# Rows of v projected behind the gated values in a one-core decoder trunk, with the long convolution's taps beside them

## The reference

```
mod = silu(c) @ w_ada + b_ada                  # six vectors: shift, scale, gate, twice
h = rms_norm(x) * (1 + sc1) + sh1
q, k, v, B, C, D = split(h @ w_in)             # nine column groups of 256
ya = differential attention(q, k, v)           # q and k normalised in groups of 32
val, gate = B;  yb = silu(layer_norm(causal_dwconv(val * sigmoid(gate), 31 taps)))
bg, cg, xc = C; yc = bg * causal_dwconv(cg * xc, 3 taps)
yd = multiscale causal pooling(D) @ w_pool * scale
x = x + g1 * (concat(ya, yb, yc, yd) @ w_out)
x = x + g2 * (relu(rms_norm(x) * (1 + sc2) + sh2) @ w_ff1) ** 2 @ w_ff2
```

## Time and profile before

| | |
|---|---|
| median of 3 runs | 2356.99 us (2356.3 to 2362.84) |
| profiled execution | 2356.43 us |
| its span | 2354.6 us |
| TensorE busy | 2283.8 us (97%) |
| VectorE busy | 1746.0 us (74%) |
| ScalarE busy | 971.2 us (41%) |
| POOL busy | 357.9 us (15%) |
| mean granted TensorE clock | 0.993 of 2.4 GHz |

### The profile page before, as it was taken

The page is one execution under the profiler, slowest core; times in us unless marked ns, Lnnn a source line. Parts: engine busy times, 40 slices in busy tenths (PEclk is TensorE's granted clock), DMA queues, the critical chain, the costliest instruction groups (busy, mean ns, idle before and its releaser), DMA issues.

```text
span 2354.6 us, 31383 instructions
## 1 busy us (share of the span) xinstructions
PE 2283.8 (97%) x11642; PEld 1924.3 (82%) x11642; DVE 1746.0 (74%) x2659; ACT 971.2 (41%) x1595; POOL 357.9 (15%) x285
## 2 busy tenths in 40 slices
PE   6999999988999999999999999999999999999999
PEld 5987898767889888888888888888888888888887
DVE  6648886889989876876767767676787676767676
ACT  4531555458888844332323232233432323222231
POOL 0442044824356610000000000000000000000000
PEclk9999999989999999999999999999999999999999
DMA  7441533120000152011111111145111111111112
GB/s 270 155 152 63 157 129 118 63 89 28 15 10 24 52 155 81 18 54 54 53 53 53 37 61 45 54 132 189 63 36 53 54 36 62 45 53 53 53 53 89
DMA packets 108280, 177.68 MB, mean 75 GB/s; under 512 B 5512, under 2 KB 77468, under 8 KB 107164
## 3 DMA queue, kind: packets, MB, share of 16 engines
q1 hardware_dynamic: 108100, 176.41, 22.6%
q10 hardware_dynamic: 88, 0.04, 0.0%
HBM read 152.84 MB, written 23.59 MB: 75 GB/s over the span
## 4 chain that ended last, share of the span: by engine, by line
PE 81%; DVE 10%; DMA 3%; issue 2%; ACT 2%; POOL 2%; SPq 0%; ACTq 0%; DVEq 0%; POOLq 0%
PE ps L2513 10%; PE ps L2512 10%; PE ps L2511 10%; PE ps L2550 8%; PE ps L2548 8%; PE ps L2549 8%; PE ps L2210 5%; PE ps L2212 5%; PE ps L2211 5%; PE ps L2401 3%; DVE ps L1615 2%; PE ps L2458 2%; PE ps L2456 2%; PE ps L2457 2%; DMA sb_w_raw<-in_w_in 2%
## 5 line engine op out<-in xcount | busy, mean ns | idle before, releaser
L1997 DVE TENSOR_TENSOR sb_x_new<-sb_x_new,ps 128x512 f32<-128x512 f32 x512 | 347.2, 684 | 107.5 <-PE ps L2513 102.0
L2511 PE MATMUL ps<-sb_w_hi,sb_u_hi 128*128 128x512 f32 x1024 | 398.3, 389 | 0.0
L2512 PE MATMUL ps<-sb_w_lo,sb_u_hi 128*128 128x512 f32 x1024 | 398.3, 389 | 0.0
L2513 PE MATMUL ps<-sb_w_hi,sb_u_lo 128*128 128x512 f32 x1024 | 398.3, 389 | 0.0
L2512 PEld LDWEIGHTS ps<-sb_w_lo,sb_u_hi 128*128 128x128 f32 x1024 | 192.2, 188 | 39.9
L2511 PEld LDWEIGHTS ps<-sb_w_hi,sb_u_hi 128*128 128x128 f32 x1024 | 192.2, 188 | 39.9
L2513 PEld LDWEIGHTS ps<-sb_w_hi,sb_u_lo 128*128 128x128 f32 x1024 | 192.2, 188 | 39.9
L2212 PE MATMUL ps<-sb_h_hi,sb_w_lo 128*128 128x512 f32 x512 | 199.4, 389 | 0.0
L1428 ACT ACTIVATE ps<-ps 128x512 f32<-128x512 f32 x28 | 16.3, 582 | 410.8 <-PE ps L2550 410.8
L2210 PE MATMUL ps<-sb_h_hi,sb_w_hi 128*128 128x512 f32 x448 | 177.5, 396 | 0.7 <-DVE sb_w_lo L1958 0.7
L2211 PE MATMUL ps<-sb_h_lo,sb_w_hi 128*128 128x512 f32 x448 | 174.4, 389 | 0.0
(11 more groups left out here) (291 smaller groups left out, 4947.9 us busy)
## 6 DMA issues: line engine op xcount, KB each, us to landing
sb_w_full<-in_w_ff SPq DMA_DIRECT2D x34, 1024.0 KB, 4.9
sb_w_full<-in_w_ff SPq DMA_DIRECT2D x56, 512.0 KB, 3.7
sb_w_raw<-in_w_in SPq DMA_DIRECT2D x16, 1024.0 KB, 5.6
sb_ada<-in_w_ada SPq DMA_DIRECT2D x32, 512.0 KB, 5.0
sb_ada_first<-in_w_ada SPq DMA_DIRECT2D x8, 1024.0 KB, 13.7
sb_x_in<-in_x SPq DMA_DIRECT2D x16, 512.0 KB, 5.4
sb_mix_in<-mix_scratch SPq DMA_DIRECT2D x16, 512.0 KB, 4.9
sb_x_new<-in_x SPq DMA_DIRECT2D x16, 512.0 KB, 4.9
```

What stands on the lines that cost most here:

```text
L1997: V.tensor_tensor(out=y, in0=y, in1=psum[:, 4 + p % 4, :], op=ALU.add).then_inc(ff2_read, 1)
L2511: M(dst, uh, wh[:, j, col], start=j == order[0], stop=False, skip_group_check=fast)
L2512: M(dst, uh, wl[:, j, col], start=False, stop=False, skip_group_check=fast)
L2513: ins = M(dst, ul, wh[:, j, col], start=False, stop=j == order[1], skip_group_check=fast)
```

## The change

The rows of v are no longer projected between the tiles of q and k. In each half they form a stage of eight tiles between val and ud, and the order of items, banks, staging buffers and stores follows. VectorE's taps are moved: two instead of five behind each tile of the row stage, 30 beside the v stage, fewer later, and none in the attention. ScalarE's `make_taps` of block 0 stand between its copies of v, POOL's `add_taps` of block 0 before the pooling windows. ScalarE moves the first convolution block in the middle of cg.

```diff
-ITEMS = [("q", Q0), ("k", K0), ("v", V0), ("gate", GATE0), ("val", VAL0), ("ud", UD0),
+ITEMS = [("q", Q0), ("k", K0), ("gate", GATE0), ("val", VAL0), ("v", V0), ("ud", UD0),
          ("cg", CG0), ("xc", XC0), ("bg", BG0)]
...
-            out += [("qk", h, t, 0), ("qk", h, t + 1, 0), ("v", h, t, 0)]
-        for kind in ("gate", "val", "ud", "cg", "xc", "pool", "bg"):
+            out.append(("qk", h, t, 0))
+        for kind in ("gate", "val", "v", "ud", "cg", "xc", "pool", "bg"):
+            if kind == "v":
+                out += [("v", h, t, 0) for t in range(0, HT, 2)]
+                continue
...
                     if t >= 2:
-                        store_turn(n - 2)
+                        store_qk(n - 2)
...
                 load_w_in(w0 + 7)
+                for t in range(0, HT, 2):
+                    store_v(h, t)
                 load_ada(h, 7)
...
                 modulation(h, 6)
+                if h:
+                    add_taps(0, 0, SHARED_NO[1])
                 for b in range(NB):
...
-            add_taps(0, 0, SHARED_NO[1])
...
                 if h:
                     begin_sum(0)
+                copy_v(h, 0)
+                if h:
                     make_taps(0, 0, 4)
+                for t in range(2, HT, 2):
+                    copy_v(h, t)
+                    if h and t < HT - 2:
+                        make_taps(0, 2 + t, 4 + t)
+                if h:
+                    make_taps(0, HT, SHARED_NO[1])
...
-                each_block("cg", h, to_gated(ACT.Copy))
+                each_block("cg", h, to_gated(ACT.Copy), (lambda: None) if h else (lambda: move_conv(0, 0)))
...
                     else:
-                        pump(taps, 5)
+                        pump(taps, 2)
...
-                    if (cc, b) == (0, 1):
-                        w_in_tail(w0 + 6)
-                pump(taps, 3)
+                w_in_tail(w0 + 6)
+                pump(taps, 30)
...
-                pump(taps, 20)
+                pump(taps, 16 if h else 20)
...
-                        pump(taps, 4 if (cc, b) == (0, 0) and h == 0 else 6)
+                        pump(taps, 4 if h or (cc, b) == (0, 0) else 6)
...
-                    if h or b == 0:
-                        pump(taps, 3)
+                    if b == 0:
+                        pump(taps, 2 if h else 3)
...
-                if h == 0:
+                if h:
+                    pump(taps, 1)
+                else:
...
-                pump(taps, 4 if u < 3 else 9 * TAPS)
...
-                    if t == 1:
-                        item_ready(w0 + 2)
-                    if t in (1, HT - 1):
-                        project_v(h, t - 1)
-                    if t and t != HT - 2:
-                        ins = project_v(h, t)
-                        if t % 2:
-                            ins.then_inc(proj_ready, 1)
-                for i, kind in enumerate(("gate", "val", "ud", "cg")):
-                    project_cols(kind, h, w0 + 3 + i)
+                project_cols("gate", h, w0 + 2)
+                project_cols("val", h, w0 + 3)
+                item_ready(w0 + 4)
+                for t in range(HT):
+                    ins = project_v(h, t)
+                    if t % 2:
+                        ins.then_inc(proj_ready, 1)
+                project_cols("ud", h, w0 + 5)
+                project_cols("cg", h, w0 + 6)
```

More of the change, by code:

```diff
@@ L464, in used @@
             h, i = divmod(w, NI)
-            if i < 3:
-                last = ("v", h, HT - 2, 0) if i == 2 else ("qk", h, HT - 1, 0)
+            if i < 2:
+                last = ("qk", h, HT - 1, 0)
+            elif ITEMS[i][0] == "v":
+                last = ("v", h, HT - 2, 0)
             else:
@@ L472, in qk_turn @@
         def qk_turn(n):
-            return n // 2 * 3 + n % 2
+            return n + n // HT * HT // 2
         def v_turn(h, t):
-            return (h * HT + t) // 2 * 3 + 2
+            return (h + 1) * HT + h * HT // 2 + t // 2
         def slot_of_qk(n):
@@ L674, in _ @@
                         load_ada(h, t // 2)
-                store_turn(h * HT + HT - 2)
+                store_qk(h * HT + HT - 2)
                 load_ada(h, 4)
                 load_w_in(w0 + 4)
-                store_turn(h * HT + HT - 1)
+                store_qk(h * HT + HT - 1)
                 load_w_in(w0 + 5)
@@ L1165, in _ @@
                         h_head(n + 1 + h, h_tmp)
-                    if t >= 2 and t % 2 == 0:
-                        copy_v(h, t - 2)
                     if t == 0:
@@ L1179, in _ @@
                 qk_root(h * HT + HT - 1)
-                copy_v(h, HT - 2)
                 scale_ada(h, 4)
@@ L2308, in project_v @@
                     free(o)
-                return project_rows(h, t, h * NI + 2, bank(o)[:, t % 2 * GW:(t % 2 + 1) * GW])
+                return project_rows(h, t, h * NI + 4, bank(o)[:, t % 2 * GW:(t % 2 + 1) * GW])
             def next_tile(n):
```

7 lines of the change are left out of this document (removed).

## The result

| | before | after |
|---|---|---|
| time, median (lowest to highest), 4 runs each | 2357.8 us (2356.3 to 2362.8) | 2378.9 us (2377.8 to 2381.0) |
| profiled execution: time, span | 2356.4, 2354.6 us | 2377.9, 2376.1 us |
| TensorE's mean granted clock in it | 0.993 | 0.987 |

The changed kernel takes 1.0088 times as long, with a 95% interval of 1.0076 to 1.01: 21 us slower. The forecast was 2371, with 2360 to 2380 as its range.

What follows compares the result with a forecast made beforehand. TensorE was taken as the bound in the first half's projections, so added idle time counts one for one: 10.4 + 4.1 + 5.7 + 1.5 - 2.4 - 4.5 = +14.8 on 2356.4, giving 2371.2 us; range 2360 to 2380.

Steps and rivals of the forecast that it cites:

- Row stage, first half, +10.4: q,k tiles without v: a cycle of waits through four engines sets the pace, not TensorE; +10.4 us, bounds 8 and 12.
- walk: First half's row stage, tile by tile: tile 6 starts at 90.1, tile 7 at 97.2, ending at 103.0.
- the ring: First half's row stage: x landing, q,k normalisation, POOL gains and sums, next loads; 17.6 us per two tiles, TensorE wants 13.3.
- Row stage, second half, +4.1: Second half's q,k tiles: 5 us idle instead of 1 at one tile, 1.4 more at another; +4.1 us, bounds 2 and 6.
- The mean, +5.7: Layer norm's mean in gate, second half: modulation chain covered only by gate blocks, 7.2 us idle; +5.7 us, bounds 4.5 and 6.5.
- Columns, -2.4: Second half, val to the short convolution's products: VectorE gains 7.8 us, so TensorE's 2.1 us wait and small ones go; -2.4 us.
- Attention, -4.5: Attention's start: VectorE drops nine taps and two sums, 7.2 us, of which 4.5 count; at least 2.5, at most 7.2 + 1.6.
- Clock: +1.5 us: New idle pieces of 5 and 7 us bring a low TensorE clock again; one such piece taken, +1.5 us, range 0 to 6.
- Rival 4: The clock falls in every waiting tile: five more tiles at 1.7 us, 2371 + 8 = 2379; chance 0.12.
- Rival 1: First half's loads of x are not late, so 6.5 us of idle pieces vanish: 2364.7; chance 0.16.
- rival 2: Faster: modulation weights don't hold TensorE, row stages run at 6.63 us per tile: 2349.5 to 2351.5; chance 0.08.
- Rival 3: Attention gives back all it takes (8.8 us), row stage costs its low bounds: 2359.7, no difference; chance 0.12.

Runs made afterwards that it cites:

- experiment 9: Changed kernel with x loaded before modulation weights (first half), convolution's sum moved first and gate's weights two tiles later (second half): 2359.7 us.
- experiment 3: Changed kernel with ScalarE moving the convolution's sum ahead of its scaling of the fifth modulation weights, second half: 2372.8 us.
- experiment 4: Changed kernel with nine of the second half's taps and two closing sums put back into attention: 2378.3 us, ratio to before 1.0074.
- experiment 5: Kernel before, v left between the row tiles, with only attention's nine taps made ahead of it: 2368.3 us (before 2357.3).
- experiment 7: Kernel before, delayed by twelve clears of a tile ahead of its first transfer: 2369.4 us (before 2357.8).
- experiment 1: Changed kernel with SyncE issuing modulation weights one tile later, behind the load of x, in the first half's row stage: 2371.1 us.
- Experiment 2: Changed kernel with GpSimd's sums cut to 64 of each 1024 columns, modulation not summed in full: 2363.6 us (before 2359.0).

## Why the prediction came out as it did

- **Direction and range: right.** Slower had 0.78 (its named parts, 0.52, 0.12 and three quarters of 0.16, add up to 0.76); the time lies 8 us above the number, near the upper end.
- **Row stage, first half, +10.4: the mechanism is right, the sum 3 us short**, above its bound of 12 (13.4 and 13.6 us with the later first point). The low part of tile 6 and so its matmuls came at 91.58 (walk: 90.1), since the ring took 18.9 us, not 17.6, all of it the landing (6.76 us instead of 5.4). VectorE's own step to tile 7 took 8.55 us, not 7.1, because two of its operations are stretched beside GpSimd's sums. So tile 7 started at 100.13 (97.2) and the end came at 105.96 (103.0). That only 6.7 us of this stage's 12.6 are idle and 5.9 are clock doesn't speak against the walk: the low clock lies under VectorE's pace.
- **Row stage, second half, +4.1: near in size** (4.8 and 5.3, of which 3.1 and 1.7 are idle time), its cause only in part. The wait came where I had put it, 4.59 us for 5. But experiment 9 took it and all of the stage's loss out by moving gate's weights, whose split stood in VectorE's and ScalarE's queues in front of a later tile's x. I had costed their new turn at nothing in the first half ("they take v's former turn") and not looked at it in the second.
- **The mean, +5.7: right** (5.0 and 4.9), and experiment 3 takes 4.2 of it away by order alone. The 1.8 us of low clock behind it had no price.
- **Columns, -2.4: right.** The wait of 2.1 us is gone; the clock took 2.0 back in one pair, 0.6 in the other.
- **Attention, -4.5: size off, reason wrong.** I had priced VectorE's taps as waiting of TensorE. Waiting fell by 1.6 and 1.2 us, and experiment 4 puts at most 0.35 us of it on the taps; with the taps out and v left in place (experiment 5) it did not fall at all. The first stage gained 6.6 and 3.5 us, mostly clock, and the stage behind it lost 5.6 and 2.8: over the whole attention 1.0 and 0.8 us are left of 4.5. Over all profiles attention as a whole took 347.3 to 354.0 us with the taps out and v moved (nine, mean 349.4), 349.3 to 356.1 with the taps in (four, mean 352.4), so that a gain of some 3 us would fit them too. The first stage's busy time was 21.1 us in three profiles of the kernel before and 19.4 in experiment 4, against 16.1 to 19.1 without the taps; what ties the low clock to them isn't shown.
- **"Everything behind is not touched": true of instructions and waits** (idle +0.1), not of the time.
- **Where the missing 7 us are.** Against a forecast of +14.8 the spans differ by 21.5 and 21.6. The first half's row stage is 3.0 and 3.2 us above its term, attention as a whole 3.5 and 3.7, the columns 2.3 and 0.9 (all clock), the second half's row stage 0.7 and 1.2, the mean 0.7 and 0.8 below. These stages hold their low clock, so the term of 1.5 for it, and the 0.5 by which the end of the first pair is shorter, come off again.
- **"Clock: +1.5 us" was too small, and how much it cost is known only as a bound.** Outside the first half's row stage busy time grew by 4.1 and 4.7 us, and in that stage the clock added 0 and 1.5. So 4 to 6 us is the most that the clock cost, at the upper end of the 0 to 6 that I gave; the part of it that is hidden under the second half's wait isn't known. My sentence that it costs nothing where the next wait is already there is what the first half showed: 5.9 us of low clock, and none of it on top.
- **Rival 4**, the clock that falls in each waiting tile, named 2379 and came nearest, but by luck. Its mechanism is there: 0.83 and 0.66 in the first row stage, each in the slice behind a wait. Its price isn't: in the first half these low clocks were hidden under VectorE's pace, and what its 8 us stood for were the landing, VectorE's step and attention. By the Trainium skill (TensorE: Matmul & The Clock Gate, HAM oscillation — how this bites in real kernels) a wait in every tile can bring the low clock back each time; the trace of after agrees, with granted clocks of 0.83 and 0.66 behind its two waits.
- Why the stage behind the second layer-norm sum has more low clock in both pairs stays open. Its length varies by more than that between profiles, and experiment 7 excludes the later start.
- Rival 1 falls by the x worked on at 86.26 and by experiment 1, rival 2 by the ring's 18.9 us. Rival 3 falls with attention's gain, 1 us where it had 8.8.

The Trainium skill (SBUF — State Buffer, Who interferes with whom) says that where a VectorE and a GpSimd instruction both want the port pair that they share, the one that is issued first keeps it for its whole length and the other is blocked. I used this for GpSimd's 128x256 operation and overlooked the other side, which is the dearer one: beside a pair of GpSimd's sums VectorE's two operations took 2.0 and 1.45 us more. The trace of before had the first of them already:

```profile
95.96 2.18 DVE L1480 SCALAR_TENSOR_TENSOR sb_stat<-sb_stat 128x1 f32<-128x1 f32 x1
```

The scaling of x came there after the sums, at 101.21, and took 0.75 us. Experiment 2 agrees with the rule: with the two sums cut to 0.59 us together both operations are back at 0.39 and 0.75.

## What to carry to other kernels

Work moved away from a stage uncovers what was sized for the longer stage: look at each in-order queue for a transfer that stands in front of a more urgent one, and for weights that keep a turn which nobody needs any more. Here three such orders (x behind modulation weights, a copy behind a scaling, gate's weights in v's turn) cost 19 us together (17 by the changed kernel's second median), nearly all that the change cost. Price each new idle piece of TensorE with its clock, but only as far as no other engine sets TensorE's next start: here half of the added time shows as low clock, and most of that of the first half cost nothing. A walk through every engine's queue, not TensorE's idle time, gives the sum there. And split a difference by idle and busy time, in two profiles of each kernel, before a cause is named: a stage without any change differed by 3% between profiles.

## What the runs showed of the hardware that was not expected

- The same 2265 matmuls between the same waits took 320.1 to 329.7 us, at mean granted clocks of 1.00 to 0.95. In the profile of after the clock stayed at 0.50 from about 850 to 862 with TensorE never idle, where in before it was at 0.93 from 836 to 840 and at 1.00 from there. What raises it in one and not in the other isn't shown.
- A 128x1 operation of VectorE (0.22 us) and the scaling of 128x1024 (0.75 us) took 2.19 and 2.20 us beside GpSimd's additions of 2.4 us each, while statistics and reductions in between kept their 0.68 us.
